# Two heads at a time: all eight fill steps first, then scores, value products and both turnings in one group

## The reference, cut to what matters

```python
# dilated attention (first block): three patterns of window and dilation, softmax of their sum
scores = einsum('bhrnqd,bhrnkd->bhrnqk', qb, kw) + bias      # bias from relative positions
p = exp(scores - logsumexp(scores)); o = einsum('bhrnqk,bhrnkd->bhrnqd', p, vw)
# sliding-window attention (second block), with a sink column in the softmax
scores = einsum('bnqkgd,bnskd->bnkgqs', qb, kb) * d ** -0.5 + slopes * distance
probs = softmax(concatenate([scores, sink]))[..., :-1]; out = probs @ vb
```

## Time and profile before

| | |
|---|---|
| median of three runs | 1249.15 us |
| the profiled execution's own time | 1246.01 us |
| its span | 1244.2 us |
| PE busy | 1152.9 us, 93% of the span |
| DVE busy | 648.4 us, 52% |
| ACT and POOL busy | 487.1 us (39%) and 492.5 us (40%) |
| mean granted PE clock | 0.965 of full speed |
| attention a1, about | 122 to 250 us of the span |
| attention a2, about | 517 to 642 us |
| attention a3, about | 650 to 750 us |

### The profile page before, as it was taken

How to read it: one execution, slowest core, us unless ns; L and a number is a source line. 1 busy time by engine, 2 the same in 40 slices (tenths; PEclk the granted TensorE clock), 3 DMA queues, 4 the chain that set the end, 5 groups by cost and what they waited for, 6 DMA issues and landing times.

```text
span 1244.2 us, 15603 instructions
## 1 busy us (share of the span) xinstructions
PE 1152.9 (93%) x5604; PEld 914.8 (74%) x5604; DVE 648.4 (52%) x1246; ACT 487.1 (39%) x814; POOL 492.5 (40%) x385
## 2 busy tenths in 40 slices
PE   6998999987898898899999988999799999989997
PEld 5776777655797676677777766887588888878886
DVE  4276887555673557366666666469443434320003
ACT  5356444374442434344433455443322222211124
POOL 4443332352313252433333142453444555534443
PEclk9999999987899999899999998999899999999999
DMA  8576565510130032434431221352233333332211
GB/s 169 137 151 143 124 134 129 143 34 1 43 94 1 22 119 77 124 109 144 142 126 35 68 68 34 103 152 68 68 101 101 98 83 89 101 102 71 98 68 68
DMA packets 114287, 116.32 MB, mean 93 GB/s; under 512 B 4817, under 2 KB 97191, under 8 KB 114228
## 3 DMA queue, kind: packets, MB, share of 16 engines
q1 hardware_dynamic: 98800, 86.58, 25.8%
q10 hardware_dynamic: 14212, 26.13, 6.8%
q0 software_dynamic: 1216, 2.83, 0.8%
HBM read 113.41 MB, written 2.12 MB: 93 GB/s over the span
## 4 chain that ended last, share of the span: by engine, by line
PE 77%; DVE 8%; issue 5%; ACT 4%; POOL 3%; DMA 1%; SPq 0%; ACTq 0%; DVEq 0%; POOLq 0%
PE bank L660 21%; PE bank L661 20%; PE bank L662 20%; POOL wlo L462 3%; PE bank L836 3%; PE bank L861 2%; PE bank L844 2%; PE bank L970 2%; PE bank L981 1%; DMA raw<-w_in 1%; ACT whi L1218 1%; PE bank L765 1%; PE bank L994 1%; DVE nhf L1670 1%; DVE att_qk L1733 1%
## 5 line engine op out<-in xcount | busy, mean ns | idle before, releaser
L462 POOL TENSOR_TENSOR wlo<-raw,whi 128x512 fp32r<-128x512 f32 x312 | 423.5, 1388 | 601.5 <-ACT whi L1218 601.5
L660 PE MATMUL bank<-h_hi,whi 128*128 128x512 f32 x984 | 407.5, 414 | 28.9 <-POOL wlo L462 16.6
L661 PE MATMUL bank<-h_lo,whi 128*128 128x512 f32 x984 | 390.2, 397 | 0.0
L662 PE MATMUL bank<-h_hi,wlo 128*128 128x512 f32 x984 | 389.3, 396 | 0.0
L660 PEld LDWEIGHTS bank<-h_hi,whi 128*128 128x128 f32 x984 | 189.2, 192 | 92.9 <-issue 37.8
L1218 ACT ACTIVATE whi<-raw 128x2048 fp32r<-128x2048 f32 (+1 forms) x79 | 150.1, 1900 | 183.3 <-PE bank L662 172.7
L662 PEld LDWEIGHTS bank<-h_hi,wlo 128*128 128x128 f32 x984 | 188.8, 192 | 41.5
L661 PEld LDWEIGHTS bank<-h_lo,whi 128*128 128x128 f32 x984 | 189.0, 192 | 40.2 <-issue 4.2
L1341 ACT ACTIVATE pT_a<-bank 128x256 f32<-128x256 f32 (+3 forms) x80 | 32.5, 406 | 196.6 <-PE bank L844 196.6
L660 PE MATMUL bank<-ffn_hi,whi 128*128 (+1 forms) x176 | 70.2, 399 | 4.1 <-DVE ffn_lo L1577 4.1
L1702 DVE SCALAR_TENSOR_TENSOR ada_acc<-ada_w,small,ada_acc 128x512 f32<-128x512 f32 x84 | 71.8, 854 | 0.4 <-DMA ada_w<-w_ada 0.4
(11 more groups left out here) (338 smaller groups left out, 1559.8 us busy)
## 6 DMA issues: line engine op xcount, KB each, us to landing
raw<-w_in SPq DMA_DIRECT2D x66, 512.0 KB, 5.7
ada_w<-w_ada ACTq DMA_DIRECT2D x96, 256.0 KB, 2.9
raw<-w_up SPq DMA_DIRECT2D x44, 512.0 KB, 4.8
raw<-w_down SPq DMA_DIRECT2D x22, 512.0 KB, 4.1
raw<-w_out SPq DMA_DIRECT2D x16, 512.0 KB, 4.4
x_tok<-x SPq DMA_DIRECT2D x4, 512.0 KB, 6.4
toe<-bias_rows POOLq DMA_DIRECT2D x8, 256.0 KB, 6.5
raw<-w_branch_swa SPq DMA_DIRECT2D x4, 512.0 KB, 3.5
```

Source lines behind the costliest of these rows:

```text
L462: ins = pool.tensor_tensor(wlo[s][:, c], raw[s][:, c], whi[s][:, c].bitcast(F32), ALU.subtract)
L660: pe.matmul(ps, wh, h_hi, start=start, stop=False)
L661: pe.matmul(ps, wh, h_lo, start=False, stop=False)
L662: return pe.matmul(ps, wl, h_hi, start=False, stop=stop)
```

## The change

In a1 and a2 (`per == 2`) the loop on PE now goes over pairs. First come the fill steps of both units (and the fold), then the scores of the next pair, the value products of the pair before, and the turnings of both units of this pair. In a3 (`per == 1`) the order is what it was. No other engine's program changes, and no instruction is added or removed.

```diff
-            def attention(tag, units, tail=None):
+            def attention(tag, units, tail):
...
-                for w in range(len(units)):
-                    if w % per == 0:
-                        for g in range(M * (w + 2), M * (w + 2 + per)):
-                            qk(g)
-
-                    if tail:
+                for w in range(0, len(units), per):
+                    if per == 2:
                         tail(w)
-                    if w >= per and w % per == 0:
+                        tail(w + 1)
+                    for g in range(M * (w + 2), M * (w + 2 + per)):
+                        qk(g)
+                    if per == 1:
+                        tail(w)
+                    if w >= per:
                         values(range(w - per, w))
-                    turn(w)
+                    for k in range(per):
+                        turn(w + k)
                 values(range(len(units) - per, len(units)))
-                if tail:
-                    for w in range(3):
-                        tail(len(units) + w)
+                for w in range(3):
+                    tail(len(units) + w)
```

## The result

| | before | after |
|---|---|---|
| median | 1249.59 us (1247.99 to 1251.21, 4 runs) | 1343.12 us (1335.55 to 1351.41, 4 runs) |
| ratio, 95% interval | | 1.075 (1.0662 to 1.0838) |
| profiled execution, its span | 1246.01, 1244.2 us | 1350.57, 1348.8 us |
| a1, from its first scores to its last value product | 128.1 us | 201.8 us |
| a2, likewise | 124.3 us | 156.2 us |

The four times of the changed kernel stand in two pairs, 1335.55 and 1335.67 us at a mean PE clock of 0.951 and 0.950, and 1350.57 and 1351.41 at 0.932 and 0.931; which of the two a run takes was not tried, and the profile is of the second pair, some 7 us above the median.

The account below looks back on a forecast made before the run. PE was taken to bound a1 and a2. Stalls 47 + 26, GpSimd 4 and clock 24, less 8 saved, made 93 us on 1246.0, so 1339, or 1343 us as median; range 1305 to 1372.

Parts of the forecast that it names:

- The mechanism: In a1 and a2, VectorE takes the next scores and does tail before the second probabilities, so PE's second turning waits.
- The signs: Profile after: turning waits near 75 us in about 30 times, longest about 4; a1 grows about 60 us, a2 30.
- The stalls: PE standing still for what its other work leaves uncovered of VectorE's chain: 47 us in a1, 26 in a2.
- the sum: 47 + 26 + 4 + 24 - 8 = 93 us on the profiled 1246.0; as a median 1343 us, 7.5% slower.
- the pairs that the sum lists: a1's pairs by key blocks: stalls of 3.0 to 3.8 us with taps, 1.2 to 2.2 in pairs 12 to 14.
- the one without value products: Pair 0 of a1, with no value products to cover its chain: 1.0 us added to its stall of 3.0.
- GpSimd's share: VectorE's `ada` slowed beside GpSimd's low part in about 14 chains, 0.3 us each: 4 us, ends 0 and 15.
- The clock: PE's clock falls behind all twelve stalls with taps and 3 of 18 shorter ones, 1.6 us each: 24 us.
- The case without any fall: Rival: the clock doesn't fall in dense fill work, so the sum lacks its 24 us: 1319 us; chance 0.20.
- The saving: Fewer tile shape changes on PE, 0.17 to 0.3 us in 30 pairs, plus 1 us of old waits: 8 us.
- the sentence on what VectorE's tail holds up: In a1 and a2, VectorE does `tail(2k)` and only then makes `probs(2k+1)`, for which PE's turning waits.

Follow-up runs that it names:

- the kept-busy kernel: Changed kernel plus matmuls nobody reads before the second turning's wait, 6 in a1's first twelve pairs, 2 in the others: 1316.69 us, ratio 1.0541.
- the first one with the tail between the probabilities: Changed kernel with VectorE's order in a1 and a2 as even probabilities, even tail, odd probabilities, both next scores: 1242.95 us, ratio 0.9948.

## Why the prediction was right, point by point

- **The mechanism** was right: VectorE's scores and tail ahead of the second probabilities. Putting the scores back (1253.5) takes nearly all of the loss away, and so does changing VectorE's order alone, with PE's left as it is (1243.0). The signs came as named: 69.7 us of waits in 32 times, the longest 3.7 (75, about 30 and 4 in the prediction), a2 longer by 31.9 us (30), and the rest of the span within 1 us. a1 grew by 73.7 us in the slower execution, where 60 was named, and its mean clock was 0.79, where 0.87 was.
- **The stalls** were 47 + 26 in the sum, and are 47.1 + 27.3 by starts of matmuls, without the 1.9 us of the last pair of a1, which was there before. In a1 the pairs that the sum lists held to 0.15 us each (the one without value products, 4.0 against 3.87, is the farthest), in a2 to 0.3.
- **GpSimd's share** was 4 us in the sum, for `ada` in about 14 chains. The trace has it in three, in a2, at 618, 656 and 695 us, where `ada` took 1.00 us under GpSimd's low part in place of 0.74; in the chains of a1 it took 0.75 each time. So it was 0.8 us, and the term was too large:

```profile
616.09 2.50 POOL L462 TENSOR_TENSOR wlo<-raw,whi 128x512 fp32r<-128x512 f32 x2
...
618.14 1.00 DVE L1703 SCALAR_TENSOR_TENSOR ada_acc<-ada_w,small,ada_acc 128x512 f32<-128x512 f32 x1
```

- **The clock** was 24 us in the sum, and is 26 us (medians, with PE kept busy) to 40 (the profiled executions). The length was too low: I counted 3.4 us for each fall, and in a1 ten of the twelve were 6.8. So was the number of falls at the short stalls, 3 forecast and 8 seen. By the balance of the medians, with the saving as forecast, it is 93.5 - 74.4 + 8 = 27 us. The case without any fall (1319) is where the kept-busy kernel landed, 1316.7.
- **The saving** of 8 us can't be seen in the changed kernel itself. Where nothing waits it is 0.27 us a pair, in the forecast's 0.17 to 0.3. Between the kernel before and the first one with the tail between the probabilities, whose PE order is the changed kernel's, it is 6.3 us (0.5%), and that one still has 2.8 us of waits in units 8, 16 and 24.
- **That the sum hit the median to 0.1 us is luck.** The changed kernel's own times are 16 us apart, the clock's term was too small by 2 us or more, and GpSimd's too large by 3.
- **What I had wrong without its showing in the number** is the sentence on what VectorE's tail holds up. I named the probabilities as its only consumer on PE. The fill tile's bank is one as well, and with the first door out of the way it holds PE for three quarters as long (31.1 us in twelve waits, against 42 us of stalls at the same places). It cost nothing in the changed kernel, as the first door covers it, and it made two of my later forecasts miss, by 59 us and by 72 to 77.

## What to carry to other kernels

When a producer is moved next to a consumer, list what the engine between them does in its own order between the two, not only the work on the data itself: here 3 of 5 us were taps and a multiplication for somebody else. Then ask for every consumer of these pieces, since the one that shows in the profile hides the next. An order on one engine has to be chosen together with the order on the other: the grouping lost 7.5% with VectorE's old order, and gained 0.5% with one that puts its side work under the fill steps.

## What the runs showed of the hardware that I had not expected

- PE's clock fell 2.0 to 2.6 us into ten of the twelve long stalls of a1, while PE still waited, and stayed down for 6.8 us, so that more than 5 us of each of these falls were paid in matmuls 0.43 us apart in place of 0.23. Short stalls fell on both sides: one of 1.9 us that ended at 601 us of the span had a fall behind it, one of 1.9 us that ended at 641 us had none. With matmuls that nobody reads in the stall (2.6 of 3.8 us) it stayed at 0.99 and 1.00. The Trainium skill ("TensorE: Matmul & The Clock Gate", "What's actually happening") has "activity releases the throttle", and this trace agrees.
- A matmul's row ends some 0.2 us after the next could begin, so a wait in the profile is shorter by that than the time lost: 69.7 us in the rows of the turnings' waits, 76.3 us by starts.
- Of the waits that PE had for two semaphores, one was named after GpSimd, whose work ended 0.14 us after VectorE's and was not what the matmul needed.
